# HGRN2 and S5 block on one core: weight sums by accumulating DMAs in DRAM, sines and cosines made in the input-value stage, and the order matrices, then states on VectorE

## The chip, the cores and the metric
The kernel runs on 1 core of one Trainium2 chip. The metric is the device time of one execution in microseconds, the median of several. PE is TensorE, DVE VectorE, ACT ScalarE, POOL GpSimd and SP SyncE, which issues most of the DMAs.

## What is computed (the reference, cut)
One layer over 2048 tokens of width 1024. `u` is the normalised input, one product with `w_in` gives all projections, and two token mixers run on them.
```python
u = rms_norm(h, norm_g[l])
proj = u @ w_in[l]
q, f_logit, iv, g_hg, u_s, z_s, gate_hg, gate_s5 = jnp.split(proj, _split_points(), axis=-1)
o = hgrn2_mix(q, f_logit, iv, lb_all[l])            # 8 heads, a recurrence over chunks of 64 tokens
ys = s5_mix(u_s, a_re, a_im, log_dt, b_re, b_im, c_re, c_im, d)   # 32 groups of 16 channels
# s5_mix: dt = exp(log_dt); lr, li = exp(ar*dt) * cos(ai*dt), exp(ar*dt) * sin(ai*dt)
#         x = u B;  h_t = (lr + i li) h_{t-1} + x_t;  y = Re(C h) + D u
merged = sigmoid(gate_hg) * y_hg + sigmoid(gate_s5) * y_s5
h = h + merged @ w_out[l]                            # then a second gated product, and the last norm
```

## The kernel before
Products are made of 128 x 512 matmuls; each factor is split into a rounded high part (ACT, "round") and the rest (DVE, "split"), and one product takes three matmuls for each 128 rows of the sum: hi x hi, hi x lo, lo x hi. The stages, by time in the trace:

- **Normalisation** and the S5 inputs, to about 116 us.
- **Input values**, 116 to 282 us. `iv_rows` on PE makes 32 rows of products (2 x TOKENS), into eight banks in turn; ACT drains row i (`drain_iv`). Beside it DVE builds the "terms" (`recover`, `combine`): sums and differences of u's quarters, which POOL stores to DRAM from the two buffers in `w.raw`. Then the weights of head 0 are loaded into the same `w.raw`, rounded and split.
- **Recurrence**, 284 to 928 us: 8 heads x 4 tiles = 32 steps (`head`). Step n projects tile n on PE and carries through the recurrence of step n - 1. At its end DVE's `gate` writes the output y, one buffer of 128 x 512; POOL stores it (`o_gated`), and the next `gate` waits until that store has landed (`o_out`).
- **Quad stage** (`part_s5`), 928 to 1510 us: the z and gate columns of `w_in`. Two blocks of columns by two tiles of tokens make a unit; there are NQ = 20 units (10 pairs of blocks, for tiles 0 and 1, then for 2 and 3). A unit has PRODS = 7 products in place of 8, over half the rows each, by sums and differences of quarters of both factors (Winograd's form). The factors of u are the terms. Those of the weights are three quarters as they are and four sums S1 to S4, "pieces" of 128 x 512. Product i of unit u uses piece q = 7u + i; pieces live in a ring of four. `piece(u, i)` on ACT and on DVE rounds and splits piece 7u + i + 4, four products ahead.
- **Tail**, 1510 us on: the output projections.

In the quad stage each unit from 2 to 17 also makes one pair p = u - 2 of S5 groups (MAKE), units 3 to 18 use it (USE), and units 4 to 19 do its GELU. For a pair: DVE `matrices` (17 dependent instructions: X, the input matrix, and Z, the output matrix), PE `turn_inputs` (two transposes of X, L1464, after product 5), ACT `copy_turned`, and PE `states_in` after product 6 (L1473 and L1477). In the next unit DVE `taps` (the matrix within a chunk), `turn_back` (inputs times cos and sin), `scans`, `turn_forward` (back, into Hp), and PE `outputs` (L1490, L1493) at the unit's end.

What makes the sums and the angles before: POOL. `sum_s3`, `sum_s1_s2` and `sum_s4` add quarters in SBUF for each unit, and `angles` makes 10 dependent instructions for each pair, from whose result ACT's `sine` makes one pair's sines and cosines in one buffer. SP loads the weights of unit u + 1 as two blocks in three DMAs (`load_block_a`, `load_block_b_low`, `load_block_b_high`), each after `sums_done` of unit u.

The order is written out by hand, engine by engine, and every hand-over is a semaphore. Every DMA of SP, and every one of POOL, waits behind the ones issued before it on the same engine. At the change from unit 9 to unit 10 the seven terms of the second half are loaded in place of those of the first, 1 MB each, as their last products are done.

## Time and profile before
| | |
|---|---|
| median of 3 timed runs | 2290.68 us (2288.84 to 2298.66) |
| the profiled execution | 2278.27 us |
| its span | 2276.5 us |
| mean granted clock of PE | 0.973 |
| busy: PE, DVE, ACT, POOL | 95%, 71%, 47%, 19% |
| weight loads on PE (PEld) | 78% |
| moved by DMA | 258.05 MB, 113 GB/s |

The shares are means over stages with different limits. The stages are read one at a time: the busy time of each engine in a stretch, the granted clock beside it, and who waited for whom.

### The profile page before, as it was taken

The numbers are of one execution on the slowest core, as the hardware profiler recorded it, in microseconds if no ns is written. First come the engines' busy times: TensorE is split into PE (matmuls) and PEld (weight loads), VectorE is DVE, ScalarE is ACT, GpSimd is POOL, SyncE is SP. The second block draws the span as 40 slices with busy tenths as digits, with TensorE's granted clock in tenths as the row PEclk, the third lists the DMA queues.
The fourth block names the chain that finished last, engine by engine and source line by source line (L and its number), as shares of the span: only waits on it lengthen the run. The fifth ranks groups of instructions, "written<-read, shape, count | busy, mean of one in ns | idle before, by whom it ended". The sixth has DMA issues, their size and how long they took to land.

```text
span 2276.5 us, 29105 instructions
## 1 busy us (share of the span) xinstructions
PE 2161.8 (95%) x10178; PEld 1765.0 (78%) x10178; DVE 1606.1 (71%) x2995; ACT 1069.3 (47%) x1603; POOL 435.1 (19%) x533
## 2 busy tenths in 40 slices
PE   9999999999999999878887788889999999999997
PEld 7788888888888888666665666668888888888886
DVE  7671077778777877768888797846567666756756
ACT  6511145545555554544446454443364354445335
POOL 0010000000000000256666566621101200200100
PEclk9999999999999999999998898999999999999999
DMA  6463211101111111232326222256536634733732
GB/s 214 109 217 117 88 43 52 56 23 55 53 35 41 55 46 50 82 100 96 105 92 201 92 95 96 91 158 221 168 100 195 219 105 154 243 120 120 226 125 74
DMA packets 161326, 258.05 MB, mean 113 GB/s; under 512 B 40576, under 2 KB 95616, under 8 KB 161216
## 3 DMA queue, kind: packets, MB, share of 16 engines
q1 hardware_dynamic: 137680, 182.42, 25.4%
q0 software_dynamic: 23536, 74.22, 9.1%
q8 instruction: 63, 1.03, 0.2%
q14 instruction: 47, 0.39, 0.1%
HBM read 188.27 MB, written 67.11 MB: 112 GB/s over the span
## 4 chain that ended last, share of the span: by engine, by line
PE 79%; DVE 13%; issue 2%; ACT 2%; DMA 2%; POOL 1%; SPq 1%; DVEq 0%; ACTq 0%; POOLq 0%
PE c_bank L340 22%; PE c_bank L341 22%; PE c_bank L342 22%; PE c_bank L1453 2%; PE c_bank L1455 2%; PE c_bank L1454 2%; DVE c_w_both L259 2%; PE c_bank L732 1%; PE c_bank L709 1%; PE c_bank L719 1%; PE c_bank L730 1%; DVE s_xt L1764 1%; DVE s_Z L1732 1%; PE c_bank L1490 1%; PE c_bank L1493 1%
## 5 line engine op out<-in xcount | busy, mean ns | idle before, releaser
L340 PE MATMUL c_bank<-u_hi,c_w_both 128*128 128x512 f32 x576 | 231.8, 402 | 1.9 <-DVE u_lo L1105 1.0
L342 PE MATMUL c_bank<-u_hi,c_w_both 128*128 128x512 f32 x576 | 224.3, 389 | 0.0
L341 PE MATMUL c_bank<-u_lo,c_w_both 128*128 128x512 f32 x560 | 218.6, 390 | 0.0
L2239 ACT ACTIVATE c_w_both<-c_raw 128x1024 fp32r<-128x1024 f32 x91 | 96.6, 1061 | 161.5 <-PE c_bank L342 154.8
L987 DVE STREAM_TRANSPOSE hg_ken<-hg_ke 32x128 f32<-32x128 f32 x512 | 154.8, 302 | 6.5
L1453 PE MATMUL c_bank<-u_hi,c_w_both 128*128 128x512 f32 x280 | 121.4, 433 | 16.9 <-ACT s_stage L1523 12.1
L585 POOL DMA_DIRECT2D o_gated_scratch<-hg_y x31 | 16.8, 542 | 629.6 <-DVE hg_y L1029 629.6
L340 PEld LDWEIGHTS c_bank<-u_hi,c_w_both 128*128 128x128 f32 x576 | 108.2, 188 | 32.4 <-issue 5.5
L340 PE MATMUL c_bank<-t_oa_hi,c_w_both 128*128 128x512 f32 (+1 forms) x344 | 132.2, 384 | 0.0
L341 PE MATMUL c_bank<-t_oa_lo,c_w_both 128*128 128x512 f32 (+1 forms) x344 | 132.2, 384 | 0.0
L342 PE MATMUL c_bank<-t_oa_hi,c_w_both 128*128 128x512 f32 (+1 forms) x344 | 132.2, 384 | 0.0
L342 PEld LDWEIGHTS c_bank<-u_hi,c_w_both 128*128 128x128 f32 x576 | 108.2, 188 | 23.0
L1523 ACT ACTIVATE s_stage<-c_bank 128x512 f32<-128x512 f32 x80 | 47.7, 596 | 162.0 <-PE c_bank L1455 162.0
L799 ACT ACTIVATE hg_S<-hg_G,hg_coef 128x128 f32<-128x128 f32 x120 | 47.5, 401 | 160.6 <-DVE hg_G L1012 114.7
L341 PEld LDWEIGHTS c_bank<-u_lo,c_w_both 128*128 128x128 f32 x560 | 105.3, 188 | 19.5 <-issue 0.2
L1453 PE MATMUL c_bank<-u_lo,c_w_both 128*128 128x512 f32 x280 | 118.0, 422 | 0.3 <-issue 0.3
L1454 PE MATMUL c_bank<-u_lo,c_w_both 128*128 128x512 f32 x280 | 117.4, 419 | 0.0
L1455 PE MATMUL c_bank<-u_hi,c_w_both 128*128 128x512 f32 x280 | 117.3, 419 | 0.0
L2384 DVE TENSOR_TENSOR c_w_both<-c_raw,c_w_both 128x1024 fp32r<-128x1024 f32 x91 | 110.9, 1219 | 7.5 <-ACT c_w_both L2239 7.5
L1454 PE MATMUL c_bank<-u_hi,c_w_both 128*128 128x512 f32 x280 | 114.0, 407 | 0.0
L1455 PE MATMUL c_bank<-u_lo,c_w_both 128*128 128x512 f32 x280 | 113.9, 407 | 0.0
L340 PE MATMUL c_bank<-u_hi,hg_wq 128*128 128x512 f32 x256 | 102.3, 400 | 0.0
(386 smaller groups left out, 6013.7 us busy)
## 6 DMA issues: line engine op xcount, KB each, us to landing
c_raw<-w_in_in SPq DMA_DIRECT2D x44, 512.0 KB, 4.1
gates_scratch<-s_stage POOLq DMA_DIRECT2D x64, 256.0 KB, 3.0
t_ein<-gates_scratch SPq DMA_DIRECT2D x64, 256.0 KB, 4.4
c_raw<-w_o_hg_in SPq DMA_DIRECT2D x32, 512.0 KB, 3.5
c_raw<-w_out_in SPq DMA_DIRECT2D x32, 512.0 KB, 3.5
c_raw<-w_ple_gate_in SPq DMA_DIRECT2D x32, 512.0 KB, 3.3
terms_scratch<-c_raw POOLq DMA_DIRECT2D x24, 512.0 KB, 3.0
c_raw<-w_in_in SPq DMA_DIRECT2D x44, 256.0 KB, 3.6
```

The costliest lines, as they stand in the source:

```text
L259: dve.tensor_tensor(lo, self.piece(q), hi.bitcast(F32), ALU.subtract).then_inc(self.piece_lo.sem, 1)
L340: pe.matmul(out, w_hi, u_hi, start=first, stop=False)
L341: pe.matmul(out, w_hi, u_lo, start=False, stop=False)
L342: return pe.matmul(out, w_lo, u_hi, start=False, stop=last)
L799: act.activation(S[:, p], G[:, (p + 1) % 2], ACT.Copy, scale=coef[:, 2 * p:2 * p + 1]).then_inc(states, 1)
L987: ins = dve.transpose(ken[j * SQ:(j + 1) * SQ, :, i * SQ:(i + 1) * SQ], ke[i * SQ:(i + 1) * SQ, :, 1 + j // 2, j % 2 * SQ:(j % 2 + 1) * SQ])
L1453: pe.matmul(out[:], hi[:, kk_], b_hi[:, k, at], start=start, stop=False, skip_group_check=True)
L1454: pe.matmul(out[:], hi[:, kk_], b_lo[:, k, at], start=False, stop=False, skip_group_check=True)
L1455: ins = pe.matmul(out[:], lo[:, kk_], b_hi[:, k, at], start=False, stop=stop, skip_group_check=True)
L1523: act.activation(stage[:, s], bank[:], ACT.Copy).then_inc(snapped.sem, 1)
L2239: act.activation(w_hi[u % WS], raw[u % RS], ACT.Copy).then_inc(w_hi_done, 1)
L2384: dve.tensor_tensor(w_lo[u % WS], raw[u % RS], w_hi[u % WS].bitcast(F32), ALU.subtract).then_inc(w_lo_done, 1)
```

## The change
Four things are changed together.

1. **Sums in DRAM.** The four sums of each of the ten pairs of blocks are made once and kept in DRAM (`sums`). POOL issues, in head 0 of the recurrence, 40 DMAs from DRAM to DRAM that copy a quarter of `w_in` each (`begin_sums`), and 40 accumulating ones that add another quarter, or a sum, to it (`add_to_sums`), each of 128 x 512. Each group waits until the one before has landed. The quad stage loads each piece by its own DMA, from `w_in` or from `sums`, into a ring of four in `w.raw` (`load_piece`). Thus POOL computes nothing in that stage.
2. **Sines and cosines** of all 16 pairs are made in the input-value stage: nine dependent DVE instructions a pair after the terms, one ACT instruction between drains, a store by POOL (256 KB) into `trigs`. In the quad stage SP loads one pair per unit, into two buffers in turn. ACT's `sine`, with its table load, goes from there. The loads and roundings of head 0's first weights come two rows later on ACT and wait on SP for the last of these stores.
3. **DVE's order** within a unit: `taps`, `matrices`, `turn_back`, `scans`, `turn_forward`, in place of `taps`, `turn_back`, `scans`, `turn_forward`, `matrices`, with the pieces between them.
4. **SP's order**: terms 2 and 3 are loaded around pieces 4 to 7, ahead of unit 0's other loads, and at unit 9 one term after each piece.

```diff
@@ class Quads
-    def load_block_a(self, sp, u):
-        if u:
-            sp.wait_ge(*self.sums_done.at(4 * u))
-            sp.wait_ge(*self.piece_lo.at(PRODS * (u - 1) + 2))
-        sp.dma_start(self.w.raw[:, 0], self.a["w_in"][self.blocks(u)[0]]).then_inc(self.a_in.sem, 16)
...
+    def load_piece(self, sp, q):
+        u, i = divmod(q, PRODS)
+        if q >= PRODS * NQ:
+            return
+        if q >= 4:
+            sp.wait_ge(*self.piece_lo.at(q - 3))
+        if i in self.SUM_OF:
+            src = self.a["sums"][self.SUM_OF[i], PAIR_ORDER[u % 10]]
+        else:
+            src = self.a["w_in"][self.blocks(u)[i == 6], :, HALF_KT:] if i else self.a["w_in"][self.blocks(u)[0], :, :HALF_KT]
+        sp.dma_start(self.piece(q), src).then_inc(self.piece_in[q % 4].sem, 16)
...
+    def begin_sums(self, pool):
+
+        for s, (row, half) in enumerate(((1, 0), (0, 0), (0, 0), (0, 1))):
+            for j in range(NQ // 2):
+                src = self.a["w_in"][ZB + 2 * j + row, :, half * HALF_KT:(half + 1) * HALF_KT]
+                pool.dma_start(self.a["sums"][s, j], src).then_inc(self.sums_kept, 16)
+
+    def add_to_sums(self, pool, s):
+        for j in range(NQ // 2):
+            src = {self.S1: self.a["w_in"][ZB + 2 * j + 1, :, HALF_KT:], self.S3: self.a["w_in"][ZB + 2 * j + 1, :, :HALF_KT],
+                   self.S2: self.a["sums"][self.S1, j], self.S4: self.a["sums"][self.S2, j]}[s]
+            pool.dma_start(self.a["sums"][s, j], src, accum_op=ALU.add, max_dma_last_dim=2048).then_inc(self.sums_kept, 16)
...
+    def keep_trig(self, pool, p):
+        out = self.angle_buffers()[3][p % 2]
+        pool.wait_ge(*self.trig_made.at(p + 2))
+        pool.dma_start(self.a["trigs"][p], out).then_inc(self.kept[p % 2], 16)
...
+    def all_angles(self, dve):
...
+        for p in range(PAIRS):
+            sin, cos = out[p % 2][:, 0], out[p % 2][:, 1]
+            if p:
+                dve.wait_ge(*self.angle_made.at(p))
+            link(dve.tensor_scalar(t1, nn, f_hi[:, p:p + 1], None, ALU.mult))
+            link(dve.tensor_scalar(t2, t1, MAGIC, MAGIC, ALU.add, ALU.subtract))
+            link(dve.tensor_tensor(t1, t1, t2, ALU.subtract))
+            link(dve.scalar_tensor_tensor(t1, nn, f_lo[:, p:p + 1], t1, ALU.mult, ALU.add))
+            link(dve.tensor_scalar(t2, t1, MAGIC, MAGIC, ALU.add, ALU.subtract))
+            if p >= 2:
+                dve.wait_ge(*self.trig_kept(p - 2))
+            link(dve.tensor_tensor(sin, t1, t2, ALU.subtract))
+            link(dve.tensor_scalar(t1, sin, 0.25, None, ALU.add))
+            link(dve.tensor_scalar(t2, t1, MAGIC, MAGIC, ALU.add, ALU.subtract))
+            dve.tensor_tensor(cos, t1, t2, ALU.subtract).then_inc(self.angle_made.sem, 1)
@@ part_head, gpsimd
+            def add_sums(t):
+
+                if t == 0:
+                    quads.begin_sums(pool)
+                elif t == 1:
+                    pool.wait_ge(quads.sums_kept, 4 * quads.SUM_DMAS)
+                    quads.add_to_sums(pool, quads.S1)
+                    quads.add_to_sums(pool, quads.S3)
+                elif t == 2:
+                    pool.wait_ge(quads.sums_kept, 6 * quads.SUM_DMAS)
+                    quads.add_to_sums(pool, quads.S2)
+                else:
+                    pool.wait_ge(quads.sums_kept, 7 * quads.SUM_DMAS)
+                    quads.add_to_sums(pool, quads.S4)
+
             def head(h, first, last):
                 for t in range(NT - 1 if last else NT):
-                    if last and t == NT - 2:
-                        quads.sum_s3(pool, 0)
-                        quads.sum_s1_s2(pool, 0)
+                    if first:
+                        add_sums(t)
                     pool.wait_ge(y_done, h * NT + t + 1)
@@ part_s5, vector
                 if use:
                     taps()
-                    turn_back()
+                if make:
+                    matrices()
                 piece(u, 0)
                 if use:
-                    scans()
+                    turn_back()
...
                 if use:
-                    turn_forward()
+                    scans()
...
-                if make:
-                    matrices()
+                if use:
+                    turn_forward()
                 piece(u, 3)
```

How DVE's instructions stand in a unit that makes and uses a pair, in the kernel before, from the end of `scans` to the start of `matrices` (s_Hp is written by `turn_forward`, c_w_both is the ring of split pieces, s_mt and s_bb belong to `matrices`):
```order
L1764 SCALAR_TENSOR_TENSOR s_xt<-s_rho,s_xt 128x256 x2
L1784 TENSOR_TENSOR s_stage<-c_bank,s_stage 128x512
L259 TENSOR_TENSOR c_w_both<-q_sums,c_w_both 128x512
L1768 TENSOR_TENSOR s_Hp<-s_xt,s_trig 128x255
...
L1773 TENSOR_TENSOR s_Hp<-s_Hp,s_t 128x255
L259 TENSOR_TENSOR c_w_both<-c_raw,c_w_both 128x512
L1710 TENSOR_SCALAR s_mt<-s_bim,s_si 128x16
L1711 SCALAR_TENSOR_TENSOR s_bb<-s_bre,s_sr,s_mt 128x16
```
The same engine in such a unit of the changed kernel, from the end of `taps` to `turn_forward`:
```order
L1763 SCALAR_TENSOR_TENSOR s_msb<-c_ident,s_dd,c_bank 16x16
L1727 TENSOR_SCALAR s_mt<-s_bim,s_si 128x16
...
L1749 SCALAR_TENSOR_TENSOR s_Z<-s_Z,s_mt 128x144
L239 TENSOR_TENSOR c_w_both<-c_raw,c_w_both 128x512
L1772 TENSOR_TENSOR s_xt<-c_bank,s_trig 128x256
...
L1777 TENSOR_TENSOR s_xt<-s_xt,s_t 128x256
L1801 TENSOR_TENSOR s_stage<-c_bank,s_stage 128x512
L239 TENSOR_TENSOR c_w_both<-c_raw,c_w_both 128x512
L1781 SCALAR_TENSOR_TENSOR s_xt<-s_rho,s_xt 128x256 x2
L239 TENSOR_TENSOR c_w_both<-c_raw,c_w_both 128x512
L1785 TENSOR_TENSOR s_Hp<-s_xt,s_trig 128x255
```
`matrices` now follows `taps`, and the first split of the unit stands behind it. Each later part of the states stands one piece further back.

POOL's instructions from the end of the input-value stage into head 0 of the recurrence, in the changed kernel; before, hg_sT was followed by the four stores of hg_y alone:
```order
L324 DMA trigs_scratch<-c_raw 128x512 x16
L667 MEMSET hg_sT 128x512
L217 DMA sums_scratch<-w_in_in 128x512 x40
L648 DMA o_gated_scratch<-hg_y 128x512
L223 DMA sums_scratch<-w_in_in 128x512 x20
L648 DMA o_gated_scratch<-hg_y 128x512
L223 DMA sums_scratch<-sums_scratch 128x512 x10
L648 DMA o_gated_scratch<-hg_y 128x512
L223 DMA sums_scratch<-sums_scratch 128x512 x10
L648 DMA o_gated_scratch<-hg_y 128x512
```
Each store of y in head 0 now stands behind a group of these DMAs.

## Rows read from the trace of the kernel before

**Rows 1.** The page, PE's busy tenths in 40 slices
```profile
PE   9999999999999999878887788889999999999997
```

**Rows 2.** Stretches: length, busy us and instructions of each engine, granted clock, DMA share, GB/s
```profile
116.00:282.00 166.00, 166.00 (x734) 137.49 (x733) 54.99 (x133) 22.94 (x36) 12.97 (x24) 1.00 0.40 137
284.00:928.00 644.00, 644.00 (x3542) 538.68 (x3540) 504.84 (x1248) 341.70 (x548) 20.58 (x34) 1.00 0.14 47
928.00:1020.00 92.00, 71.21 (x308) 56.09 (x308) 62.94 (x120) 46.08 (x73) 36.44 (x38) 0.91 0.30 98
1020.00:1192.00 172.00, 150.06 (x661) 117.18 (x659) 149.53 (x277) 82.47 (x131) 114.32 (x122) 0.92 0.30 95
1192.00:1266.00 74.00, 52.99 (x218) 40.66 (x219) 62.04 (x97) 40.34 (x51) 43.61 (x40) 0.82 0.56 179
1266.00:1490.00 224.00, 196.61 (x875) 154.66 (x872) 188.85 (x351) 108.96 (x173) 137.69 (x150) 0.92 0.28 93
```

**Rows 3.** Waits of PE, 940 to 1530: us in total, times, longest
```profile
PE c_bank L1464 <- DVEq L1734: 68.5, 16, 12.5
PE c_bank L1453 <- ACT s_stage L1523: 12.1, 4, 5.9
...
PE c_bank L1453 <- DVE u_lo L277: 4.8, 1, 4.8
```

**Rows 4.** Stretches, PE PEld DVE ACT POOL: after a wait, unit 4, unit 18
```profile
1099.70:1103.00 3.30, 3.30 (x10) 2.66 (x9) 3.21 (x3) 1.58 (x4) 2.93 (x3) 0.55 0.01 2
...
1051.30:1079.30 28.00, 24.71 (x112) 19.36 (x111) 24.72 (x45) 13.93 (x22) 19.16 (x21) 0.94 0.25 82
...
1468.90:1490.10 21.20, 21.20 (x98) 17.15 (x97) 16.19 (x28) 11.50 (x19) 7.03 (x8) 1.00 0.33 102
```

**Rows 5.** Instructions on tile s_Z: ns min/median/max, first and last start
```profile
L1732 DVE SCALAR_TENSOR_TENSOR s_Z<-s_Z,s_mt x16: 307/1256/1302, 1012.6 to 1459.7; 128x144 f32<-128x144 f32 x16
```

**Rows 6.** Timeline of PE, DVE and SP in units: start us, us, instruction
```profile
1104.05 1.08 PE L1473 MATMUL c_bank<-s_U,s_w_in_t 128*64 128x256 f32 x8
...
1105.49 1.14 PE L1490 MATMUL c_bank<-s_Hp,s_Z 64*128 64x256 f32 x8
...
1107.78 0.26 DVE L1745 COPY s_msb<-c_bank 16x112 f32<-16x112 f32 x1 [1.14 <-PE c_bank L1493]
...
1108.74 0.42 DVE L1755 TENSOR_TENSOR s_xt<-c_bank,s_trig 128x256 f32<-128x256 f32 x1
...
1109.09 5.12 SPq L1313 DMA_DIRECT2D s_w_intra<-s_msb  x8
...
1215.91 0.23 DVE L1715 TENSOR_TENSOR s_bbq<-s_bb,s_own 128x64 f32<-128x64 f32 x1
...
1219.83 0.31 DVE L1732 SCALAR_TENSOR_TENSOR s_Z<-s_Z,s_mt 128x144 f32<-128x144 f32 x1
...
1258.93 0.69 PE L1464 MATMUL c_bank<-c_ident,s_X 128*128 128x128 f32 x2 [12.48 <-DVEq L1734]
```

**Rows 7.** Timeline, end of the input values; groups of DVE: busy, mean ns
```profile
256.44 2.36 DVE L973 TENSOR_TENSOR c_w_both<-c_raw,c_w_both 128x1024 fp32r<-128x1024 f32 x2 [69.72 <-ACT c_w_both L784]
...
276.62 0.60 ACT L793 ACTIVATE n_iv_stage<-c_bank 128x512 f32<-128x512 f32 x1 [4.84 <-PE c_bank L342]
...
L1660 DVE TENSOR_SCALAR s_lr<-s_tn 128x272 f32<-128x272 f32 x1 | 0.3, 301 | 0.0
```

**Rows 8.** Timeline of POOL in head 0 of the recurrence
```profile
316.60 0.55 POOL L585 DMA_DIRECT2D o_gated_scratch<-hg_y  x1 [31.99 <-DVE hg_y L1029]
...
399.15 0.54 POOL L585 DMA_DIRECT2D o_gated_scratch<-hg_y  x1 [20.31 <-DVE hg_y L1029]
```

**Rows 9.** DMA: a queue's packets, MB, share; issues, median us to landing
```profile
q0 software_dynamic: 23536, 74.22, 9.1%
...
c_raw<-w_in_in SPq DMA_DIRECT2D x44, 256.0 KB, 3.6
...
o_gated_scratch<-hg_y POOLq DMA_DIRECT2D x31, 256.0 KB, 2.7
```

More of the change, by code:

```diff
@@ new lines, in make_trig, with link @@
+    def make_trig(self, act, p):
+        out = self.angle_buffers()[3][p % 2]
+        act.wait_ge(*self.angle_made.at(p + 1))
+        act.activation(out, out, ACT.Sin, scale=TWO_PI).then_inc(self.trig_made.sem, 1)
+    def all_angles(self, dve):
+        nn, t1, t2, out, (aim, dt, turns, tn, whole, f_hi, f_lo) = self.angle_buffers()
+        n = [0]
+        def link(ins):
+            n[0] += 1
+            ins.then_inc(self.angle_step.sem, 1)
+            dve.wait_ge(*self.angle_step.at(n[0]))
+        for sem in self.kept:
+            dve.wait_ge(sem, 16 * 12)
+        dve.wait_ge(*self.angle_in.at(1))
+        dve.wait_ge(*self.trig_made.at(1))
+        link(dve.scalar_tensor_tensor(turns, aim, 0.15915494309, dt, ALU.mult, ALU.mult))
+        link(dve.tensor_scalar(tn, turns, float(SC), None, ALU.mult))
+        link(dve.tensor_scalar(whole, tn, MAGIC, MAGIC, ALU.add, ALU.subtract))
+        link(dve.tensor_tensor(tn, tn, whole, ALU.subtract))
+        link(dve.tensor_scalar(f_hi, tn, 192.0, 192.0, ALU.add, ALU.subtract))
+        link(dve.tensor_tensor(f_lo, tn, f_hi, ALU.subtract))
+        for p in range(PAIRS):
[13 more added lines that the diff above has]
+            dve.tensor_tensor(cos, t1, t2, ALU.subtract).then_inc(self.angle_made.sem, 1)
@@ L599, in gpsimd @@
             quads.all_terms(lambda g: quads.store_terms(pool, g, False) if g >= 8 else None, lambda g: quads.store_terms(pool, g, True))
+            quads.load_angles(pool)
+            for p in range(PAIRS):
+                quads.keep_trig(pool, p)
             pool.wait_ge(sigf, 1)
@@ L942, in scalar @@
                 drain_iv(i)
-                if i == 2 * TOKENS - 5:
+                if i == TOKENS:
+                    quads.step_of_angles(act)
+                if i > TOKENS:
+                    for p in range((i - TOKENS - 1) * 3 // 2, min(PAIRS, (i - TOKENS) * 3 // 2)):
+                        quads.make_trig(act, p)
+                if i == 2 * TOKENS - 3:
                     for kind in range(2):
@@ L1342, in sync @@
                     parameters()
-                if u == 9:
-                    for m_ in range(6, len(quads.TERMS)):
-                        quads.load_term(sp, m_)
+            sp.wait_ge(*quads.piece_lo.at(PRODS * NQ))
+            for n in range(2):
+                load_tail_weights(sp, n)
         def gpsimd(pool):
@@ L2557, in build @@
             u_hi = mu.sb("hi", [P, KT, SEQ], F32R)
[L2558 to L2561 removed]
+            quads = Quads(mu, a, w, u_hi, u_lo)
             head = part_head(nc, c, a, w, quads, banks, xs, u_hi, u_lo)
```

211 lines of the change are left out of this document (71 added, 140 removed).

## The prediction
> **What bounds the kernel now.** The page's slices come first: PE stands at nine tenths nearly throughout, and at seven or eight in slices 17 to 27, of 56.9 us each [rows 1]. The table of stretches says where that is. In the input values (116 to 282 us) and the recurrence (284 to 928) PE is busy all the time at clock 1.00; in the quad stage (928 to 1510) it is not, and the clock is 0.82 to 0.92 [rows 2]. There PE idles 20.79 + 21.94 + 21.01 + 27.39 = 91 us in four stretches. The waits of PE name one cause: L1464, the turn of pair p's matrix X, waits 16 times for DVE's `matrices`, 68.5 us together. L1453 waits 12.1 us for a snapshot on ACT and 4.8 for a split term [rows 3]. The idle time isn't all: in the 3.3 us after a wait at L1464 the granted clock is 0.55, which is the 1.2 GHz level and not 2.4, and 10 matmuls run where 15 would [rows 4]. So a unit lasts 28.0 us with 24.7 busy, while unit 18, which makes no pair, takes 21.2 us at clock 1.00 [rows 4].
>
> Why is DVE late? `matrices` stands behind `turn_back`, `scans` and `turn_forward`, and POOL computes beside it: the last instruction of `matrices` takes 307 ns at best and 1256 at the median [rows 5]. POOL is busy 114 of 172 us there [rows 2].
>
> **The change, part by part.** (1) The order on DVE. A unit that makes and uses a pair needs unit 18's 21.2 us of PE plus `states_in` (L1473 and L1477, 1105.49 - 1104.05 = 1.44 us [rows 6]) and two transposes (0.35, half of their row's 0.69, since matmuls overlap [rows 6]): 23.0 us if nothing waits. Can DVE keep up? Unit 18 holds all of its work but `matrices`: 16.2 us busy [rows 4]. Without POOL beside it `matrices` runs its last 12 instructions in 4.23 us (1215.91 to 1220.14) and the first five at some 0.23 each [rows 6]: 5.4. Together 21.6, under 23.0, and 16.2 still holds some of POOL's slowing. By the order, with a product at 12 x 0.226 = 2.7 us (166 us over 734 matmuls, [rows 2]): `taps` begins some 0.4 us after product 0, when the unit before has ended its `outputs`, and takes 0.96 (1107.78 to 1108.74 [rows 6]); `matrices` ends at 6.8, the split of piece 0 at 7.4, wanted by product 4 at 10.9; `turn_back` (six of 0.46) ends at 10.2, the split of piece 1 at 11.4, wanted at 13.6; `scans` 1.4, the split of piece 2 at 13.4, wanted at 16.3; `turn_forward` at 16.2, wanted by `outputs` at 19 or later. The transposes want X at 16.3 and have it since 6.8. Each slack is 2 to 3 us.
>
> (2) The sums leave POOL, so the last argument holds: POOL keeps only issues (0.54 us each, [rows 8]). On SP each unit now issues seven loads of 256 KB and one of 256 KB for the sines, each behind the split that frees its buffer, with `fill_intra`'s eight (5.1 us, [rows 6]) behind the first. A piece goes out at 7.4 us, the next after `fill_intra` at 13, landing 3.6 later [rows 9] at 16.6; ACT wants it when product 5 is done, 16.3. That is the tightest place; I charge 0.5 us a unit to it and to `gated`, 7 us for 14 units. The DMA share of 0.30 rises to about 0.45, which other stretches carry [rows 2].
>
> (3) The sum over the stage, against 28 us and more per unit: units 3 to 8 (1020 to 1192) 172 - 6 x 23.1 = 33; units 11 to 17 (1267 to 1469) 202 - 7 x 23.1 = 40. Units 0 to 2 gain 9: SP now loads term 2 ahead of unit 1's weights, so the wait of 4.8 for a term and its slow clock go; against it DVE does `parameters` and then `matrices` of pair 0 before piece 0 of unit 2, which I take to cost what unit 2's wait at L1464 gives back. Units 9 and 10 (75 us) hold the loads of seven terms, 7 MB; their 12.48 us wait at L1464 [rows 6] goes, but ACT and DVE still round and split seven terms, and each term's load now stands behind a piece on SP: 8 gained, not 29. Units 18 and 19 gain nothing. 33 + 40 + 9 + 8 - 7 = 83.
>
> (4) Sines in the input-value stage. DVE is idle for 69.72 us, from 186.7 to 256.4 [rows 7]. 16 pairs x 9 links: an immediate 128x272 operation takes 0.30 us [rows 7], a two-tensor 128x256 one 0.42 (`turn_back`'s, [rows 6]), with some 0.04 between: 3.2 to 4.1 us a pair, 51 to 66 us from about 196, when ACT's step is made. They end at 249 to 263. ACT drains row 31 at 276.6 and PE wants head 0's weights then [rows 7]; the store of the last sines and the weights' loads take some 4 us each by the nearest row [rows 9], roundings and splits 4: ready at 261 to 275. It hides, by 15 us or by 2. Cost 0, at worst 5.
>
> (5) The sums by DMA in the recurrence. POOL issues 40 copies before it stores y of step 0, 20 adds before step 1's, 10 and 10 before steps 2's and 3's, and each group waits for the one before. y has one buffer: DVE's `gate` of step s+1 waits for the store of step s, and behind `gate` stands all of DVE's next step, while PE is busy at 100%. So a late store is a stall of everything. No row has a copy from DRAM to DRAM nor an accumulating one. The nearest is POOL's queue: 9.1% of 16 engines' 2276.5 us for 74.22 MB [rows 9], 44.7 engine-us a MB, 0.73 us for 256 KB over 16 engines. The copies: 22 us at least by the issues, 29 by the queue, 59 if reading and writing share. An add reads twice: lower bound 0.73 us, twice that 1.5, four times 2.9. I take 29 and 1.5. POOL starts at 284.6; copies land at 317 (y of step 0 goes at 316.60 anyway [rows 8]); 20 adds to 350, 10 adds to 368, issues to 373, a store 2.7 us [rows 9]. `gate` of step 4 wants it at 398. No stall but perhaps 2 to 3 us at step 2. At 59 and 2.9 the chain ends at 284.6 + 62 + 61 + 32 + 8 = 448: a stall of 50. Cost taken: 3; ends 0 and 50.
>
> A rule on exactly this: the Trainium skill, "Collectives: The Full Stack", section "The bandwidth ceiling: the fold count and why AG ≠ RS ≠ AR", says that an adding step runs at half a copy's rate because it reads two sources on one ring. By it the add is the 1.5 above and the chain has 22 us to spare; by the copy's rate it would have 45. No row of this trace can show it.
>
> A second: the skill's "SBUF — State Buffer", section "SBUF: two separate sides", says GpSimd and a VectorE operation with two SBUF inputs take a shared port in turn, for a whole instruction. The rows agree: 307 and 1256 ns are a free operation and one with a POOL operation of some 1 us ahead of it. It also bears on DVE's new work while POOL issues.
>
> **Sum.** 83 - 3 = 80 us less. The profiled execution took 2278.27 us, span 2276.5; the median of the timed runs is 12.4 above. 2278 - 80 = 2198 against its own time; against the median 2211.
>
> **Rivals.** (A) Likeliest, 0.55: as above, 2211, own range 2199 to 2228.
> (B) The units end bound by something else, 0.15: DVE's splits or SP's loads come 1 to 2.5 us late per unit, the clock falls behind each wait, 14 x 2.5 = 35 lost: 2230 to 2255. For it: slacks of 0 to 3 us only, and roundings on ACT also wait for loads. Against: DVE sheds POOL's slowing.
> (C) The adds stall the recurrence, but less than the gain, 0.14: an add of 2.2 to 4.6 us costs 30 us for each us more, 2215 to 2279; taken 2245.
> (D) Slower, 0.12: the adds are slower still. The gain of 83 is gone when the chain ends 83 us after 398; with copies at 29 that is (481 - 331) / 30 = 5.0 us an add, some 52 GB/s. From 5.4 us on the kernel is slower by over 0.5%; at 8, the stall is 331 + 240 - 398 = 173 and the time 2291 - 83 + 173 = 2381. For it: thirty adds in series groups and no row of their price; against it: plain copies of that size land 2.7 us after issue, several at a time.
> (E) No change within 0.5%, 0.04: B and C together or D at its edge.
>
> **How the numbers follow.** What the timed runs tell from no change is about 0.5%, 11 us. Faster: A, B and C, 0.84, less a little of C that reaches 2279, 0.83. Same 0.05, slower 0.12. The time is A's. The range reaches to B's and most of C's times, 2196 to 2268; below lies an own gain over 94, PE's whole idle and slow time, and above D, E and the end of C, together about 0.2.
>
> **What would show it.** In the changed trace: L1464's successor waits no longer, units last 23 to 24 us at clock 1.00 and PE is busy over 97% from unit 3 to 8 and 11 to 17; the last `matrices` instruction is near 307 ns; POOL is busy under 20% there. Between units 9 and 11 some 20 us of idle stay. DVE's chain of 9 links ends before 263, and PE has no gap at 282. In the recurrence steps 2 to 4, `gate` doesn't wait for `o_gated` stores. Wrong would be: a gap of PE between 340 and 500, at its end a y store behind `sums_kept`; or waits of PE in every unit for a split, whose own wait is ACT's for a load.

## The result, and the profile after
The changed kernel takes 2183.84 us (median, 2182.49 to 2186.0), the kernel before 2289.76 on the same chip: ratio 0.9531, 95% interval 0.9505 to 0.9557, 106 us less. The profiled execution took 2182.49 us, span 2180.9, clock 0.991. Against its own time the kernel before (2278.27) lost 95.8 us.

The page's slices of PE, then the table of stretches with the columns of [rows 2] and its first five windows:

```profile
PE   9999999999999999998997999989999999999997
```
```profile
116.00:282.00 166.00, 166.00 (x734) 137.43 (x733) 108.18 (x283) 33.32 (x54) 23.70 (x44) 1.00 0.47 162
284.00:928.00 644.00, 644.00 (x3542) 538.45 (x3541) 504.96 (x1248) 341.72 (x547) 71.90 (x111) 1.00 0.29 82
928.00:1020.00 92.00, 80.24 (x362) 64.12 (x362) 64.21 (x150) 50.27 (x80) 8.31 (x18) 0.96 0.42 138
1020.00:1192.00 172.00, 159.63 (x753) 126.64 (x753) 134.38 (x304) 89.11 (x141) 23.43 (x41) 0.96 0.58 188
1192.00:1266.00 74.00, 69.68 (x325) 54.76 (x324) 65.34 (x153) 38.80 (x63) 10.10 (x18) 0.98 0.50 164
...
1213.00:1394.00 181.00, 181.00 (x864) 145.05 (x866) 147.60 (x352) 95.17 (x161) 28.46 (x49) 1.00 0.51 165
```
The input values and the recurrence are as they were: 734 and 3542 matmuls, PE never idle, although DVE now has 108 us of work in the first and POOL issues 80 more DMAs in the second. All of the gain but about 0.5 us lies in the quad stage. From 1213 to 1394 us PE is busy all the time at clock 1.00; DVE is busy 19.2 us of each unit from 11 to 17 (134.55 of 160.21 us, 1212.92 to 1373.13). The waits of PE (940 to 1420 us) no longer name the transposes (L1492, before L1464 [rows 3]):

```profile
PE c_bank L1481 <- ACT s_stage L1551: 19.3, 5, 9.3
PE c_bank L1481 <- DVE c_w_both L239: 3.8, 2, 2.8
PE c_bank L785 <- DVE hg_ken L1058: 2.5, 1, 2.5
PE c_bank L1501 <- issue: 1.1, 1, 1.1
```
The end of `outputs` marks the units. First the timeline of the kernel before at the ends of units 3, 8, 10 and 17, then that of the changed one, with unit 11 besides:

```profile
1050.64 1.13 PE L1493 MATMUL c_bank<-s_U,s_w_intra 128*128 128x256 f32 x4
...
1191.74 1.13 PE L1493 MATMUL c_bank<-s_U,s_w_intra 128*128 128x256 f32 x4
...
1266.50 1.13 PE L1493 MATMUL c_bank<-s_U,s_w_intra 128*128 128x256 f32 x4
...
1468.26 1.13 PE L1493 MATMUL c_bank<-s_U,s_w_intra 128*128 128x256 f32 x4
```
```profile
1029.92 1.13 PE L1521 MATMUL c_bank<-s_U,s_w_intra 128*128 128x256 f32 x4
...
1144.35 1.13 PE L1521 MATMUL c_bank<-s_U,s_w_intra 128*128 128x256 f32 x4
...
1212.92 1.13 PE L1521 MATMUL c_bank<-s_U,s_w_intra 128*128 128x256 f32 x4
1235.81 1.13 PE L1521 MATMUL c_bank<-s_U,s_w_intra 128*128 128x256 f32 x4
...
1373.13 1.13 PE L1521 MATMUL c_bank<-s_U,s_w_intra 128*128 128x256 f32 x4
```
So up to the end of unit 3 20.7 us are gained, in units 4 to 8 141.1 - 114.4 = 26.7, in 9 and 10 74.8 - 68.6 = 6.2, in 11 to 17 201.8 - 160.2 = 41.6: 95.1. An undisturbed unit is 22.89 us (1212.92 to 1235.81).

On POOL in head 0 (timeline of POOL; in brackets what it waited for) the copies have landed at 323.80, 39.3 us after the first issue, the first 20 adds 32.6 us after theirs, the next 10 after 19.5, and the last is issued at 384.4. No wait stands behind the last 10:

```profile
284.46 21.05 POOL L217 DMA_DIRECT2D sums_scratch<-w_in_in  x40
316.51 0.56 POOL L648 DMA_DIRECT2D o_gated_scratch<-hg_y  x1 [11.01 <-DVE hg_y L1100]
323.80 16.86 POOL L223 DMA_DIRECT2D sums_scratch<-w_in_in  x20 [6.73 <-DMA sums_scratch<-w_in_in]
...
356.39 8.59 POOL L223 DMA_DIRECT2D sums_scratch<-sums_scratch  x10 [15.14 <-DMA sums_scratch<-w_in_in]
...
375.85 8.57 POOL L223 DMA_DIRECT2D sums_scratch<-sums_scratch  x10 [10.29 <-DMA sums_scratch<-sums_scratch]
```
The four stores of y in head 0, issued at 316.51, 337.01, 361.66 and 381.10, land 7.6, 19.9, 14.7 and 12.5 us later (2.7 in the kernel before): the second and the third half a microsecond after the adds issued ahead of them. The second lands at 356.9, where `gate` starts at 357.04; for the third, at 376.4, `gate` waits (timeline of DVE), and the fourth lands at 393.6, before the `gate` of 396.90. The first line below gives the landing times of all stores of y from 300 to 420 us:

```profile
DMA to landing us min/median/max: 2.7/10.0/19.9
```
```profile
376.49 0.75 DVE L1098 SCALAR_TENSOR_TENSOR hg_y<-c_bank,c_hg_g,hg_osq 128x512 f32<-128x512 f32 x1 [0.35 <-DMA o_gated_scratch<-hg_y]
```

### The profile page after: what moved, and what is told of

Read it like the earlier page. It is cut to its first block, busy times and chain, and to the rows that moved or that the text cites. A ratio compares the mean times of both kernels' runs of the same rounds, so it can differ in the third digit from the quotient of the medians.

```text
span 2180.9 us, 29116 instructions
## 1 busy us (share of the span) xinstructions
PE 2129.6 (98%) x10178; PEld 1745.2 (80%) x10178; DVE 1562.4 (72%) x3143; ACT 1047.9 (48%) x1589; POOL 226.1 (10%) x392
## 3 DMA queue, kind: packets, MB, share of 16 engines
q0 software_dynamic: 33872, 99.41, 14.5%
## 4 chain that ended last, share of the span: by engine, by line
PE 91%; DVE 3%; ACT 2%; DMA 2%; issue 1%; SPq 1%; DVEq 0%; POOL 0%; ACTq 0%
PE c_bank L389 23%; PE c_bank L391 23%; PE c_bank L390 22%; PE c_bank L1481 5%; PE c_bank L1482 5%; PE c_bank L1483 5%; PE c_bank L785 1%; PE c_bank L798 1%; PE c_bank L775 1%; PE c_bank L796 1%; PE c_bank L1518 1%; PE c_bank L1521 1%; DMA u_hi<-terms_scratch 1%; PE c_bank L1501 1%; DVE hg_ken L1058 0%
## 5 line engine op out<-in xcount | busy, mean ns | idle before, releaser
L389 PE MATMUL c_bank<-u_hi,c_w_both 128*128 128x512 f32 x576 | 231.8, 402 | 2.1 <-DVE c_w_both L1227 1.1
L391 PE MATMUL c_bank<-u_hi,c_w_both 128*128 128x512 f32 x576 | 224.3, 389 | 0.0
L390 PE MATMUL c_bank<-u_lo,c_w_both 128*128 128x512 f32 x560 | 218.5, 390 | 0.0
L389 PEld LDWEIGHTS c_bank<-u_hi,c_w_both 128*128 128x128 f32 x576 | 108.2, 188 | 32.6 <-issue 5.6
L1481 PE MATMUL c_bank<-u_hi,c_w_both 128*128 128x512 f32 x280 | 113.9, 407 | 17.8 <-ACT s_stage L1551 14.0
L239 DVE TENSOR_TENSOR c_w_both<-c_raw,c_w_both 128x512 fp32r<-128x512 f32 x140 | 94.9, 689 | 40.0 <-ACT c_w_both L234 36.2
L1481 PE MATMUL c_bank<-u_lo,c_w_both 128*128 128x512 f32 x280 | 113.2, 404 | 6.3 <-ACT s_stage L1551 5.3
L1482 PE MATMUL c_bank<-u_lo,c_w_both 128*128 128x512 f32 x280 | 111.1, 397 | 0.0
L1483 PE MATMUL c_bank<-u_hi,c_w_both 128*128 128x512 f32 x280 | 110.8, 396 | 0.0
L1483 PE MATMUL c_bank<-u_lo,c_w_both 128*128 128x512 f32 x280 | 110.4, 394 | 0.0
L1482 PE MATMUL c_bank<-u_hi,c_w_both 128*128 128x512 f32 x280 | 110.4, 394 | 0.0
```

The source lines that it names most:

```text
L239: dve.tensor_tensor(lo, self.piece(q), hi.bitcast(F32), ALU.subtract).then_inc(self.piece_lo.sem, 1)
L389: pe.matmul(out, w_hi, u_hi, start=first, stop=False)
L390: pe.matmul(out, w_hi, u_lo, start=False, stop=False)
L391: return pe.matmul(out, w_lo, u_hi, start=False, stop=last)
L1481: pe.matmul(out[:], hi[:, kk_], b_hi[:, k, at], start=start, stop=False, skip_group_check=True)
L1482: pe.matmul(out[:], hi[:, kk_], b_lo[:, k, at], start=False, stop=False, skip_group_check=True)
```

## The experiments
Four groups of kernels, each beside the kernel before on its own chip. That kernel's median there was 2286.78 (group 1), 2293.32 (2), 2286.27 (3) and 2279.67 (4), so the ratio is the safer number when groups are compared; the changed kernel has 0.9531 (0.9505 to 0.9557), and 0.01 of ratio is some 23 us.

### Group 1: which of the parts gains?
**Order alone**, on the kernel before:
```diff
                 if use:
                     taps()
-                    turn_back()
+                if make:
+                    matrices()
                 piece(u, 0)
                 if use:
-                    scans()
+                    turn_back()
...
```


> The kernel before with one part of the change alone: VectorE's order matrices then states. POOL still computes the sums and the angles, SP's loads are as before. Theory P (POOL's computing beside DVE is half of the old loss): X is in time, L1464 waits no more, but DVE's work stays slowed, 16.2 us of it in a unit without matrices and some 8 for matrices, 24 to 25 together against PE's 22.9; the units last 25 to 26 us and the time is 2250 (2240 to 2262). Theory O (the order is the whole gain of the quad stage): units of 23 us, time 2205 to 2215. Theory S (the sums and their loads are the gain): the order alone gives under 10 us, 2280 or more.

Measured: 2303.98 us (2301.65 to 2306.1), ratio 1.0074 (1.0057 to 1.0091): slower by 17 us. Only the bound of theory S, 2280 or more, holds; none of the three had the order as a loss. The waits of PE, then of ACT (932 to 1420 us) say where it is:

```profile
PE c_bank L1473 <- issue: 64.1, 12, 7.4
```
```profile
ACT L1534 <- DVEq L1774: 45.8, 12, 12.0
```
X is early, as meant, and L1464 waits no more. But ACT's `sine` of this pair writes the one buffer that `turn_forward` of the last pair reads (L1774 is its end), and `turn_forward` now stands later on DVE. `sine` stands ahead of `copy_turned` on ACT, and `states_in` (L1473) waits for `copy_turned`. One unit of the timelines of ACT and of PE shows the chain: the sine's table load, `copy_turned`, `states_in`:

```profile
1299.77 1.28 ACT L1534 ACT_TABLE_LOAD   x1 [2.61 <-DVEq L1774]
...
1306.54 0.36 ACT L1547 ACTIVATE s_w_in_t<-c_bank 128x256 f32<-128x256 f32 x1
```
```profile
1307.00 1.98 PE L1473 MATMUL c_bank<-s_U,s_w_in_t 128*64 128x256 f32 x8 [5.30 <-issue]
```
`turn_forward` ends at 1299.63, so `states_in`, which waits for it too, isn't held by it directly. Between sine and `copy_turned` ACT also waits 1.71 us for one of POOL's sums. The wait has moved from the transposes to `states_in`.

**The old order**, on the changed kernel (the same diff, reversed):

> The changed kernel with VectorE's old order: taps, turn_back, scans, turn_forward, then matrices. POOL computes nothing in the quad stage. Theory P: matrices takes 5.4 us and ends at about 17 to 19 us of the unit, X is wanted at 16.3; a wait of 1 to 2 us at the transposes in each unit with a slow clock behind it, units of 24.5 to 26 us, time 2184 + 14 x 2.3 = 2216 (2200 to 2230). Theory O: the units go back to 28 us, 2184 + 14 x 5 = 2254 or more. Theory S: at most 5 us over the changed kernel, below 2190.

Measured: 2183.19 us (2181.58 to 2184.17), 0.9547 (0.9531 to 0.9563): as the changed kernel. The number is theory S's; theory P, mine, does not hold. In its timeline the last instruction of `matrices` (DVE), and the transposes (PE), stand so in unit 14:

```profile
1299.88 0.31 DVE L1749 SCALAR_TENSOR_TENSOR s_Z<-s_Z,s_mt 128x144 f32<-128x144 f32 x1
```
```profile
1300.33 0.41 PE L1492 MATMUL c_bank<-c_ident,s_X 128*128 128x128 f32 x2
```
X is ready at 1300.19 and wanted at 1300.33. In the changed kernel, in the same unit, it is ready at 1289.09 and wanted at 1298.90. With POOL quiet the old order has 0.1 us to spare and the new one 9.8; either is enough, and from 1213 to 1394 us PE doesn't wait in either. Elsewhere 0.1 us is not always enough: the old order has three waits at the transposes, 8.2 us, of which 7.8 in units 9 and 10, but its waits for a snapshot are 4 us shorter (15.3 against 19.3).

**POOL busy again** without a use: in the changed kernel, per unit, 10 adds of 128x256 and 4 of 128x512 on a buffer of its own.
```diff
+            def beside(n, width):
+                for _ in range(n):
+                    pool.wait_ge(zeroed, n_extra[0])
+                    pool.tensor_tensor(extra[:, 0, :width], extra[:, 1, :width], extra[:, 2, :width], ALU.add).then_inc(zeroed, 1)
+                    n_extra[0] += 1
...
+                if u in MAKE:
+                    beside(10, NCK)
+                if 1 <= u < NQ - 2:
+                    beside(3, TT)
                 store(u, C11)
                 store(u, C12)
+                if 1 <= u < NQ - 2:
+                    beside(1, TT)
```


> The changed kernel with work added on POOL in the quad stage, on a buffer of its own that nobody else reads: 4 adds of 128x512 in each of units 1 to 17 and 10 of 128x256 in each of units 2 to 17, as many as POOL had there before. Its results are used by nobody. Theory P: the two-input operations of DVE get slower again (the last instruction of matrices from 309 ns to some 700 or more at the median, DVE busy 22 to 24 us of a unit against 18.7); with X early by the order, a unit ends 0 to 2 us later: 2190 to 2215. Theory O: DVE may be slower but PE does not wait, under 2188.

Measured: 2257.85 us (2255.27 to 2258.5), 0.9872 (0.9856 to 0.9889): 74 us of the 106 are lost again though no wait of PE, DVE or ACT names POOL. More than theory P had. POOL is busy 59.3 of 90 us (1050 to 1140), 57.5 in the kernel before; the work is not quite the same, since six of the ten instructions of `angles` had only one tensor as input. PE (932 to 1500 us) waits for DVE: at `states_in` for the end of `turn_forward`, and 28.7 us for splits:

```profile
PE c_bank L1519 <- DVEq L1809: 30.3, 12, 3.3
```
POOL's timeline, and DVE's beside it:

```profile
1113.38 8.36 POOL L1439 TENSOR_TENSOR s_extra<-s_extra 128x256 f32<-128x256 f32 x7
```
```profile
1117.82 1.40 DVE L1805 TENSOR_TENSOR s_Hp<-s_Hp,s_t 128x255 f32<-128x255 f32 x1
...
1122.07 0.42 DVE L1808 TENSOR_TENSOR s_Hp<-s_Hp,s_t 128x255 f32<-128x255 f32 x1
```
The same operation takes 1.40 us beside POOL's adds and 0.42 once they have ended. DVE's groups (1050 to 1160 us; behind the bar: busy us, mean ns, and idle time before):

```profile
L239 DVE TENSOR_TENSOR c_w_both<-c_raw,c_w_both 128x512 fp32r<-128x512 f32 x28 | 27.2, 984 | 1.5 <-DVE s_Z L1767 0.6 <-DVE s_Hp L1808 0.6
...
L1819 DVE TENSOR_TENSOR s_stage<-c_bank,s_stage 128x512 f32<-128x512 f32 x4 | 2.8, 692 | 0.1
L1790 DVE TENSOR_TENSOR s_xt<-c_bank,s_trig 128x256 f32<-128x256 f32 x4 | 1.7, 425 | 0.1
```
A split, with both inputs in SBUF, takes 984 ns at the mean against 689 in the changed kernel; an add of the same size with one input in a bank (`c_bank`, the products' sums) keeps its 692. That agrees with the section "SBUF: two separate sides" of the Trainium skill's "SBUF — State Buffer", by which GpSimd and a VectorE operation with two SBUF inputs take the shared port in turn.

**Terms late**: `load_term(2)` and `load_term(3)` of the changed kernel behind pieces 4 to 8.
```diff
-            quads.load_term(sp, 2)
-            for q in range(4, 8):
+            for q in range(4, 9):
                 quads.load_piece(sp, q)
+            quads.load_term(sp, 2)
             quads.load_term(sp, 3)
```


> The changed kernel with SP's loads of terms 2 and 3 behind those of pieces 4 to 8, where the kernel before had them behind its block loads. One theory: the early place of the two terms is what gained in units 0 to 2; the wait of PE for a split term comes back (4 to 5 us with slow clock behind it), time 5 to 9 us over the changed kernel, 2189 to 2193. The other: units 0 to 2 gained because POOL's sums are gone from them; the time stays within 2 us.

Measured: 2188.95 us (2187.76 to 2190.27), 0.9576 (0.956 to 0.9592), 5 us more (6 more than the old order on the same chip): the first theory. PE waits 6.3 us for a split term.

### Group 2: sums, angles and order crossed
The sums by POOL with the block loads of before (f), and the angles by POOL with ACT's sine of before (h), each taken back into the changed kernel, with either order. With the block loads the kernels f also have the old places of the terms' loads, which "terms late" priced at 5 us.
```diff
@@ f1, f2
-                    quads.load_piece(sp, PRODS * u + i + 8)
+                if u < NQ - 1:
+                    quads.sum_s3(pool, u + 1)
+                    quads.sum_s1_s2(pool, u + 1)
...
@@ h1, h2
-            quads.all_angles(dve)
...
+                if u in MAKE:
+                    angles(u - AHEAD)
...
+                if u in MAKE:
+                    sine(p)
```


> The changed kernel with the four weight sums of a unit computed by POOL in SBUF again and the block loads of the kernel before, and VectorE's old order; the sines and cosines stay in the input-value stage. So against the kernel before only the angles and sines are moved. Theory P (the time that POOL computes beside DVE sets the loss): POOL computed some 15.4 us a unit before, 5.5 of it sums and 9.9 angles; with the sums alone the loss of 104 us comes down to 36%: 2184 + 37 = 2221 (2205 to 2235). Theory W (what lost was the wait of ACT and DVE for pieces whose sums POOL had not made): most of the loss is back, 2255 or more.

> As the kernel with the sums on POOL and the sines moved, but with VectorE's new order (matrices before turn_back, scans, turn_forward). Theory N (the order itself is worth nothing once POOL is quiet, and something while DVE is slowed): 5 to 20 us less than with the old order. Theory Q (in the kernel before with the new order alone the loss came from ACT's sine, which waits for turn_forward through its one buffer and stands ahead of copy_turned; here no sine is there): not slower than the old order by more than 3 us. Against both: the new order is itself harmful, 10 us or more over the old one.

> The changed kernel with the angles of each pair computed by POOL and the sines by ACT in the quad stage again, as before, and VectorE's old order; the sums stay in DRAM and each piece has its own load. Theory P: 64% of the loss is back, 2184 + 66 = 2250 (2235 to 2265). Theory W: the sums were the loss, so at most 20 us: under 2204.

> As the kernel with the angles on POOL and the sums in DRAM, but with VectorE's new order. Theory Q (the sine's wait for turn_forward): the wait of PE at states_in comes back, some 5 us in most units, and the time is 15 us or more above the old order's. Theory R (in the kernel before with the new order the loss came from the block loads, which wait for pieces that are split later in the unit): no slower than the old order.

| POOL computes | old order | new order |
|---|---|---|
| sums and angles | 2289.76 (before) | 2303.98, 1.0074 |
| sums | 2263.17, 0.9872 (0.9854 to 0.989) | 2218.62, 0.9678 (0.9661 to 0.9696) |
| angles | 2239.79, 0.9769 (0.9752 to 0.9787) | 2264.48, 0.9876 (0.9857 to 0.9894) |
| nothing | 2183.19, 0.9547 | 2183.84, 0.9531 |

Theory P misses the sums: with them alone the old order stays at 2263, 79 us over the changed kernel and not 37. Its price for the angles, 2250 (2235 to 2265), holds: 2240. Theory W is right on the sums and wrong on the angles: each alone brings back more than half of the loss, so they don't add. The new order is worth 45 us while POOL makes the sums (more than N expected), and costs 25 while ACT makes the sines (Q). The waits of PE (932 to 1500 us) in the two with the sums, ACT's in the second of these, and ACT's in the one with the angles and the new order:

```profile
PE c_bank L1517 <- DVEq L1776: 60.8, 16, 9.9
```
```profile
PE c_bank L1526 <- issue: 28.5, 15, 4.2
```
```profile
ACT c_w_both L256 <- POOL q_sums L237: 60.6, 17, 8.8
```
```profile
ACT L1510 <- DVEq L1750: 43.1, 14, 7.2
```
With the old order (first row) the transposes wait for X in each of the 16 units; with the new (second) there is a smaller wait at `states_in`, behind `copy_turned`, which stands on ACT behind a rounding that waits for POOL's sum (third row; at 1306.10 it waited 3.45 us, `copy_turned` followed at 1306.63 and `states_in` at 1307.10). The fourth is the sine's wait for `turn_forward`, as in the order alone.

### Group 3: sharing or waiting; the price of an add; unit 9
**Four adds** a unit on POOL, unused: as "POOL busy again" without its 10 smaller ones, so the work of the sums.

> The changed kernel with 4 adds of 128x512 on POOL in each of units 1 to 17, on a buffer that nobody else reads: the work of the sums without anybody waiting for it. With the sums really on POOL and the same order of VectorE the time was 2219. Theory P (sharing alone): the same loss, 2210 to 2222. Theory W (the 35 us are waits of ACT for sums that POOL had late): under 2195.

Measured: 2204.25 us (2201.53 to 2207.08), 0.9634 (0.9602 to 0.9666): between the theories. Of the 35 us that the real sums cost in the new order (2218.62 - 2183.84) 20 are sharing by the medians, 24 by the ratios. The other 10 to 15 come with the terms' old place (5) and the waits for POOL's results and the block loads; no run parts these two. A split takes 1105 ns (DVE's groups, 1050 to 1160 us):

```profile
L239 DVE TENSOR_TENSOR c_w_both<-c_raw,c_w_both 128x512 fp32r<-128x512 f32 x34 | 37.1, 1105 | 1.7 <-DVE s_Z L1765 0.6 <-DVE s_Hp L1806 0.6 <-ACT c_w_both L234 0.2
```
**Every copy and add twice**:
```diff
-        for s, (row, half) in enumerate(((1, 0), (0, 0), (0, 0), (0, 1))):
+        for s, (row, half) in enumerate(2 * ((1, 0), (0, 0), (0, 0), (0, 1))):
...
-            pool.dma_start(self.a["sums"][s, j], src, accum_op=ALU.add, ...
+            for twin in (0, 4):
+                pool.dma_start(self.a["sums"][s + twin, j], src, accum_op=ALU.add, ...
```


> The changed kernel with every copy and every accumulating DMA of head 0 issued twice, the second time into a second set of sums that nobody reads (80 copies, then 40, 20 and 20 adds). Theory T (the adds are limited by the transfers, as measured in the changed kernel: 1.63 us each for the first group, 1.95 for the later ones, copies 0.98): copies end at 363, the adds at 428, 467 and, issued, at 484; gate of step 4 wants its buffer at 398, so PE stalls some 86 us and the time is 2184 + 86 = 2270 (2245 to 2285). Theory L (a group is limited by the latency and the issues of its own chain, 0.84 us an add on POOL): copies 42 us, 40 adds 34, 20 and 20 adds 19 and 19 with some 9 for the last landing of each group: end at 284 + 51 + 43 + 28 + 17 = 423, a stall of 25, time 2209. Theory H (something else gives way): under 2190.

Measured: 2266.26 us (2263.7 to 2269.06), 0.9905 (0.9872 to 0.9937): theory T, within 4 us. POOL's timeline, the waits of PE and those of DVE (300 to 560 us):

```profile
358.16 33.63 POOL L224 DMA_DIRECT2D sums_scratch<-w_in_in  x40 [30.14 <-DMA sums_scratch<-w_in_in]
...
417.62 16.95 POOL L224 DMA_DIRECT2D sums_scratch<-sums_scratch  x20 [25.25 <-DMA sums_scratch<-w_in_in]
...
451.09 16.91 POOL L224 DMA_DIRECT2D sums_scratch<-sums_scratch  x20 [15.93 <-DMA sums_scratch<-sums_scratch]
```
```profile
PE c_bank L786 <- DVE hg_ken L1059: 74.6, 4, 36.3
```
```profile
DVE hg_y L1099 <- DMA o_gated_scratch<-hg_y: 81.5, 4, 36.8
```
40 adds take 59.5 us, 20 take 33.5: 1.49 and 1.67 us each, against 0.90 a copy (80 in 72.4). `gate` waits 81.5 us for the stores of y behind them, PE 74.6.

**Term 4 first** at unit 9. In the changed kernel ACT waits 11.0 us for term 4, which SP issues behind `fill_intra`, and PE behind it (timelines of SP, ACT and PE):

```profile
1153.12 5.15 SPq L1382 DMA_DIRECT2D s_w_intra<-s_msb  x8
1158.31 2.12 SPq L210 DMA_DIRECT2D u_hi<-terms_scratch  x4
```
```profile
1165.85 1.91 ACT L247 ACTIVATE u_lo<-u_hi 128x2048 fp32r<-128x2048 f32 x1 [11.03 <-DMA u_hi<-terms_scratch]
```
```profile
1168.39 0.76 PE L1481 MATMUL c_bank<-u_hi,c_w_both 128*128 128x512 f32 x1 [9.28 <-ACT s_stage L1551]
```
```diff
+                    if u == 9:
+                        quads.load_term(sp, 4 + i)
                     if u in USE and i == 0:
                         fill_intra(p)
-                    if u == 9:
-                        quads.load_term(sp, 4 + i)
```


> The changed kernel with one change of SP's order at unit 9: the load of term 4 ahead of fill_intra's eight DMAs and not behind them. In the changed kernel ACT waits 11.0 us for this term and PE behind it 9.3. Theory: fill_intra's 5.2 us go from that wait, 3 to 7 us less, 2177 to 2181. Rival: the next term's load or fill_intra, now later, takes its place: 2182 to 2186.

Measured: 2177.26 us (2175.71 to 2178.97), 0.9518 (0.9488 to 0.9548), 7 us under the changed kernel's median: the theory, at the far end of its range. By the ratios it is 3 us, which the intervals do not part from nothing. The trace does: units 9 and 10 take 62.5 us (1143.18 to 1205.68) against 68.6, units 11 to 17 the same 160.2. PE's longest wait in the stage is 4.4 us.

**Terms deferred**: besides, `round_term` and `split_term` of terms 4 and 5 one piece later.
```diff
-                if u == 9:
-                    quads.round_term(act, 4)
                 snapshot(u, 3, sum_d, C22)
                 piece(u, 3)
...
+                    quads.round_term(act, 4)
```


> As the kernel with term 4 first, and ACT's rounding and DVE's splitting of terms 4 and 5 one piece later each (behind pieces 3 and 4), so that pieces of the weights do not stand behind a term that is still on its way. Theory: the 9.3 us wait of PE in unit 9 goes wholly and the clock stays up, 8 to 14 us less than the changed kernel, 2170 to 2176. Rival: the terms come that much later for unit 10 and the wait moves there: 2180 or more.

Measured: 2177.9 us (2177.28 to 2178.38), 0.9517 (0.9487 to 0.9547): between the theory and the rival, and no gain over term 4 first (units 9 and 10 take 64.3 us). The 9.28 us wait is gone (0.55 is left), but `copy_turned` now stands behind a term on its way, a new wait in PE's timeline:

```profile
1174.72 1.97 PE L1501 MATMUL c_bank<-s_U,s_w_in_t 128*64 128x256 f32 x8 [8.70 <-issue]
```

### Group 4: what was still open
**Four adds, old order**:

> The changed kernel with 4 adds of 128x512 a unit on POOL that nobody reads, and VectorE's old order. With the new order it took 2204. Theory M (the new order is a margin of some 10 us for X, which counts once DVE is slowed): matrices ends late for the transposes, a wait there in each unit with a slow clock, 25 to 45 us over the new order: 2229 to 2249. Theory V (the 45 us between the orders with the sums really on POOL came from the waits for sums, which fall otherwise in the old order): within 10 us of the new order, under 2214.

Measured: 2251.05 us (2249.26 to 2252.68), 0.9871 (0.9854 to 0.9889), 47 us over the new order by the medians and 54 by the ratios: theory M, a little beyond its range. Its waits of PE:

```profile
PE c_bank L1508 <- DVEq L1767: 49.7, 15, 7.9
```
The ratio is that of the kernel with the real sums in the old order, 0.9872. So in that order four adds that nobody reads cost as much as the sums with their hand-overs, block loads and late terms: by the ratios sharing is all of it. (By the medians the two lie 12 us apart, on chips where the kernel before lies 14 apart.)

**Terms early in the kernel before** (`load_term(2)` and `(3)` ahead of the loop over units):

> The kernel before with one part of the change: SP loads terms 2 and 3 ahead of the blocks of unit 1. One theory: the wait of 4.8 us for a split term and the slow clock behind it go, 4 to 7 us less than before, as the late place cost 5 in the changed kernel. The other: with POOL computing, unit 1's blocks are now late for POOL's sums and the wait moves there: within 2 us of before.

Measured: 2276.39 us (2267.6 to 2284.15, 10 runs), 0.9974 (0.996 to 0.9989): 2.5 to 9 us less by the ratio's interval, 3.3 by the medians. The wait for a split term is gone from the trace. It leans to the first theory; the size stays unsure.

**`copy_turned` first** in unit 9, and terms 5 and 6 later still:
```diff
+                if u in MAKE:
+                    copy_turned(p)
                 if u == 9:
-                    quads.round_term(act, 6)
-                if u in MAKE:
-                    copy_turned(p)
+                    quads.round_term(act, 5)
```


> As the kernel with terms 4 and 5 deferred, but in unit 9 ACT does copy_turned ahead of the rounding of term 5, and terms 5 and 6 are rounded and split one piece later. There PE waited 8.7 us at states_in for copy_turned. Theory: that wait goes and 5 to 9 us of time with it, 2169 to 2173. Rival: the seven terms are rounded too late for unit 10, the wait moves to product 1 or 2 of unit 10: 2176 to 2182.

Measured: 2178.6 us (2176.06 to 2179.96), 0.9558 (0.9541 to 0.9575): the rival. `states_in` waits 0.21, and a wait of 8.00 us for a snapshot stands at 1181.49, ahead of the third product of unit 10. Units 9 and 10 take 63.5 us. Two orders of ACT only moved the wait; the earlier load is what helped.

## Why the prediction was wrong
The sign and rival A were right; the time lies 27 us under the forecast and 12 under the range. Two terms of the sum were mis-sized, a bound was misread, and the mechanism named first was not the one:

- **"(3) The sum over the stage."** To the marks above I had 14.5 us up to unit 3 (9 and a sixth of 33), 27.5 for units 4 to 8, 8 for 9 and 10, 40 for 11 to 17, less 7 of friction and 3 in the recurrence: 80. The trace has 20.7, 26.7, 6.2, 41.6, 0 and 0: 95.1. The unit (23.0 forecast, 22.89 found) was right, and units 9 and 10 within 2 (PE idles 68.57 - 51.88 = 16.7 us there, forecast some 20). The **friction was a term without a wait behind it**: SP was called the tightest place, yet PE never waits at all in units 4 to 8 and 11 to 17. **Up to unit 3** 6 us more are gained. The 9 for units 0 to 2 were the late terms alone, and these cost 5 (terms late). The rest is waits that the sum held to be unchanged or cancelled: to the end of unit 3, those for a snapshot fell from 9.0 to 4.7 us, and 6.9 at the transposes and 2.2 at `states_in` went. No run shows which part of the change did that.
- **"below lies an own gain over 94, PE's whole idle and slow time"** made the range too tight below. To the end of unit 18's `outputs` (first the kernel before, then the changed one):

```profile
928.00:1491.33 563.33, 472.20 (x2059) 369.71 (x2059) 464.69 (x844) 278.04 (x427) 333.38 (x350) 0.91 0.33 106
```
```profile
928.00:1395.45 467.45, 439.00 (x2056) 349.00 (x2056) 366.70 (x842) 245.94 (x395) 62.31 (x112) 0.97 0.52 167
```
Idle alone was 91 us, and the same matmuls now take 33 us less: 124 at least. The bound had the idle time and almost none of the slow clock's.
- **"The median of the timed runs is 12.4 above."** I carried that over as if it belonged to the kernel. The changed kernel's median is 1.4 above its profiled execution: 11 of the 27 us. In all groups together the kernel before ran from 2276 to 2299 us, its medians from 2279.67 to 2293.32 by chip, and the profiled execution isn't one of the timed runs; a single execution of it is no anchor to half a per cent. Whether the chip makes the difference, and why it scatters more than the changed one (2182 to 2186, on one chip), was not tried.
- **"(1) The order on DVE"** was given first place. Alone it costs 17 us, and without it the change takes 2183 all the same. What the prediction said of POOL under (2), "so the last argument holds", carries most of the gain: with POOL quiet X is in time in either order, and adds that nobody reads bring 74 us back in the new order (fourteen a unit) and 67 in the old (four), by the ratios 78 each of 107. Of what is left the terms' place (5) and waits for POOL's results are known; the rest is open. The order is a margin of 9.7 us more for X, worth 45 to 54 while POOL makes sums or adds, nothing when POOL is quiet, and a loss of 17 and 25 where ACT makes the sines. The sine's one buffer, which makes it harmful there, was in no rival.
- **The signs forecast for the stage** came: POOL busy 28.46 of 181 us, PE 100% in units 4 to 8 and 11 to 17, the last instruction of `matrices` near 307 ns ([rows 5]; now 308 at the median). DVE's work was put too high, 21.6 us a unit against 19.2: unit 18's 16.2 us are 13.8 with POOL quiet.
- **"(4) Sines in the input-value stage"**: the last store goes at 256.19 and PE has no gap at 282. Cost 0, right.
- **"(5) The sums by DMA"**: copies 39 us where 29 were taken, an add 1.63 in the first group and 1.95 in the second where 1.5 was; the chain's last issue ends at 384.4 against 373. The step that failed here is "a store 2.7 us": behind copies and adds a store takes 7.6 to 19.9 us, because it lands only with what was issued ahead of it. So the spare time isn't the 22 us forecast, nor the 11 from 384.4 and 2.7 to 398, but 0.1 us at the `gate` of step 2, none at step 3 (it waits 0.35) and 3.3 at step 4. PE did not wait, so the cost was 0, against 3 taken; how late `gate` may be before PE waits was not tried. That it came out as 0 was in part luck. Rivals C and D had the mechanism right: with everything doubled the stall comes, 82 us.

The Trainium skill's rule in "Collectives: The Full Stack", section "The bandwidth ceiling: the fold count and why AG ≠ RS ≠ AR" (an add at half a copy's rate), is stated there for a reduce-scatter between cores. For these DMAs on one core it is near: 1.63 / 0.98 = 1.7 for adds from `w_in`, 1.95 / 0.98 = 2.0 for those between sums, 1.49 / 0.90 = 1.7 and 1.67 / 0.90 = 1.9 with twice as many.

## What to carry to other kernels
When two engines share a port, count what leaves it before what is reordered, and undo each part of a bundled change alone: here the order looked like the cause and was worth nothing, or less than nothing, by itself. Put back only the work that was taken away, with nobody waiting for it, to tell sharing from waiting. Before an instruction is moved later, list what waits for its end, buffers as well as results. An allowance for friction needs a wait in a row behind it, a bound on a gain has to hold the slow clock's time beside the idle time, and a median needs more than one profiled execution to stand on. A small store behind large DMAs of the same engine is to be counted at their landing, not at its own.
